# The heads' projection of a two-block model on one core: six accumulation banks filled slice by slice, and the vector engine's side work in another order

## What is computed

```python
y_b = hgrn2_mixer(p[..., o1:o2], p[..., o2:o3], p[..., o3:o4], p[..., o4:o5], lower_bounds[l], hgrn_norm_g[l])
merged = (jax.nn.sigmoid(p[..., o5:o6]) * (y_a @ w_ssm_proj[l])
          + jax.nn.sigmoid(p[..., o6:]) * (y_b @ w_hgrn_proj[l]))
```

## Time and profile before

| what | value |
|---|---|
| median of the runs | 3601.41 us |
| the profiled execution, its own time | 3603.62 us |
| span of the profiled execution | 3601.8 us |
| TensorE matmul busy | 3289.2 us, 91% |
| VectorE / ScalarE / GpSimd busy | 56% / 26% / 6% |
| mean granted TensorE clock | 0.946 of full |
| stage `heads_out`, first to last matmul | 933.15 to 1056.39 us |

### The profile page before, as it was taken

The page is one execution under the profiler, slowest core; times in us unless marked ns, Lnnn a source line. Parts: engine busy times, 40 slices in busy tenths (PEclk is TensorE's granted clock), DMA queues, the critical chain, the costliest instruction groups (busy, mean ns, idle before and its releaser), DMA issues. The chain is left out here.

```text
span 3601.8 us, 47693 instructions
## 1 busy us (share of the span) xinstructions
PE 3289.2 (91%) x20158; PEld 3042.2 (84%) x20158; DVE 2008.2 (56%) x2814; ACT 943.8 (26%) x1178; POOL 227.4 (6%) x224
## 2 busy tenths in 40 slices
PE   3999999999688779999999999899988996988887
PEld 3999999999677679999999999899988983555465
DVE  5565655566568444566446446645445535666446
ACT  3222222222323331121111111221133314444323
POOL 0000000000005200000000000000012000222200
PEclk9999999999798789999999999999989997999898
DMA  3222222222343344321321321411121321000031
GB/s 100 91 78 75 90 85 86 90 89 74 137 102 50 95 170 135 129 77 53 106 81 46 108 79 38 153 37 43 50 74 37 128 87 74 1 1 1 22 133 69
DMA packets 102463, 285.76 MB, mean 79 GB/s; under 512 B 13157, under 2 KB 32101, under 8 KB 101993
## 3 DMA queue, kind: packets, MB, share of 16 engines
q1 hardware_dynamic: 102248, 282.70, 24.6%
HBM read 218.68 MB, written 63.98 MB: 78 GB/s over the span
## 5 line engine op out<-in xcount | busy, mean ns | idle before, releaser
L491 PE MATMUL mixer_in_dense<-mix_z_high,mixer_in_whigh 128*128 128x348 f32 x1344 | 445.8, 332 | 11.3 <-POOL mixer_in_out L328 11.3
L491 PE MATMUL mixer_in_dense<-mix_z_high,mixer_in_wlow 128*128 128x348 f32 x1344 | 439.1, 327 | 0.0
L491 PE MATMUL mixer_in_dense<-mix_z_low,mixer_in_whigh 128*128 128x348 f32 x1344 | 438.2, 326 | 0.0
L1372 PE MATMUL flow_dense<-rst_norms_operand_b_high,flow_whigh 128*128 128x342 f32 x1248 | 399.2, 320 | 0.4 <-DVE flow_wlow L1464 0.4
L1372 PE MATMUL flow_dense<-irst_norms_operand_b_low,flow_whigh 128*128 128x342 f32 x1248 | 398.3, 319 | 0.0
L1372 PE MATMUL flow_dense<-rst_norms_operand_b_high,flow_wlow 128*128 128x342 f32 x1248 | 397.4, 318 | 0.0
L1930 PE MATMUL joint_dense<-rst_norms_operand_b_high,joint_whigh 128*128 128x342 f32 (+2 forms) x1056 | 344.7, 326 | 17.0 <-DVEq L2047 10.1
L1930 PE MATMUL joint_dense<-rst_norms_operand_b_high,joint_wlow 128*128 128x342 f32 (+2 forms) x1056 | 341.7, 324 | 0.0
L1930 PE MATMUL joint_dense<-irst_norms_operand_b_low,joint_whigh 128*128 128x342 f32 (+2 forms) x1056 | 340.6, 323 | 0.0
L1372 PE MATMUL flow_dense<-first_operand_a_high,flow_whigh 128*128 128x342 f32 (+1 forms) x912 | 291.4, 320 | 26.9 <-DVEq L1485 26.9
L1372 PE MATMUL flow_dense<-first_operand_a_low,flow_whigh 128*128 128x342 f32 (+1 forms) x912 | 291.8, 320 | 0.0
(11 more groups left out here) (544 smaller groups left out, 6201.3 us busy)
## 6 DMA issues: line engine op xcount, KB each, us to landing
mixer_in_wstage<-w_in SPq DMA_DIRECT2D x56, 512.0 KB, 4.6
mixer_in_mod_w<-w_mod SPq DMA_DIRECT2D x64, 384.0 KB, 3.6
first_norms_weights<-w_up SPq DMA_DIRECT2D x44, 512.0 KB, 3.5
flow_side<-h SPq DMA_DIRECT2D x24, 512.0 KB, 4.3
h<-flow_out SPq DMA_DIRECT2D x24, 512.0 KB, 3.2
first_norms_weights<-ab_w_in SPq DMA_DIRECT2D x20, 512.0 KB, 3.6
p<-mixer_in_out SPq DMA_DIRECT2D x16, 528.0 KB, 2.9
first_norms_weights<-w_down SPq DMA_DIRECT2D x16, 512.0 KB, 3.5
```

Of the source, the lines that this page charges most:

```text
L491: mm = pe.matmul(pd[s % 2][:, 0:W], a[n % 2][:, P * m:P * (m + 1)], z[x][:, m, W * b:W * (b + 1)], start=m == 0 and i == 0, stop=m == DT - ...
L1372: mm = pe.matmul(o, w[n % NW][:, P * k:P * (k + 1)], x[h][:, k, where], start=k == 0 and e == 0, stop=k == kt - 1 and e == 2)
```

## The change

It keeps every operation and changes places:

1. TensorE begins with six slices at once, the two first output tiles: for each block k it makes the three matmuls of each of the slices 0 to 5, in six banks (`RING` is 6). The slices from 6 on are made one by one, as before.
2. So `high(1)` and `low(1)` move to the front, ahead of the split of block 1, and the load of weight tile 1 moves ahead of the load of block 1. `high` and `low` of the tiles from 2 on stay where they were, `low(2)` at s = 4.
3. The table of pieces: one power behind each of blocks 4 to 6 and four behind block 7 (it was two each, and one). `turns` to `vectors` are one slice later; `table` 0 goes from s = 3 (ahead of the gate of tile 1 and of `high(2)` on ScalarE) to s = 4 (behind both), `table` 1 from s = 6 to s = 7 (behind the gate of tile 2 and `high(3)`). `outer` 1 goes from 7 to 8, `outer` 6 from 16 to 15.

```diff
-    W, NP, NQ, RING = NM // 3, NPAIR, 8, 4
+    W, NP, NQ, RING = NM // 3, NPAIR, 8, 6
...
-    for s, name, k in ((-8, "step", 0), (-7, "angles", 0), (-5, "base", 0), (-4, "power", 2), (-4, "power", 3),
...
+    for s, name, k in ((-8, "step", 0), (-7, "angles", 0), (-5, "base", 0), (-4, "power", 2), (-3, "power", 3),
...
@@ SyncE
                 for m in range(4):
                     load_yb(m)
+                    if m == 0:
+                        load(1)
                 for m in range(4, HH):
                     sp.wait_ge(x_low, m - 3)
                     load_yb(m)
-                load(1)
@@ ScalarE
                 high(0)
                 for m in range(HH):
+                    if m == 1:
+                        high(1)
...
-                        if n + 1 < DT:
+                        if n and n + 1 < DT:
                             high(n + 1)
@@ TensorE
-                for s in range(NS):
...
+                def products(s, k):
                     n, b = divmod(s, 3)
+                    for e, (w, v) in enumerate(((wh, 0), (wl, 0), (wh, 1))):
+                        mm = pe.matmul(pd[s % RING][:, 0:W], w[n % 2][:, P * k:P * (k + 1)],
+                                       x[v][:, k, FIRST + W * b:FIRST + W * (b + 1)],
+                                       start=k == 0 and e == 0, stop=k == DT - 1 and e == 2)
+                    return mm
+
+                for k in range(DT):
+                    pe.wait_ge(x_low, k + 1)
+                    for s in range(6):
+                        if k == 0 and s % 3 == 0:
+                            pe.wait_ge(low_ready, s // 3 + 1)
+                        mm = products(s, k)
+                        if k == DT - 1:
+                            mm.then_inc(full, 1)
+                for s in range(6, NS):
+                    if s % 3 == 0:
+                        pe.wait_ge(low_ready, s // 3 + 1)
+                    pe.wait_ge(moved, s - RING + 1)
                     for k in range(DT):
+                        mm = products(s, k)
                     mm.then_inc(full, 1)
@@ VectorE
                 low(0)
                 for m in range(HH):
+                    if m == 1:
+                        low(1)
...
-                    if b == 1 and n + 1 < DT:
+                    if n and b == 1 and n + 1 < DT:
                         low(n + 1)
```

More of the change, by code:

```diff
@@ L650, in heads_out @@
     at = {}
-    for s, name, k in ((-8, "step", 0), (-7, "angles", 0), (-5, "base", 0), (-4, "power", 2), (-4, "power", 3),
[L652 to L655, removed]
+    for s, name, k in ((-8, "step", 0), (-7, "angles", 0), (-5, "base", 0), (-4, "power", 2), (-3, "power", 3),
+                       (-2, "power", 4), (-1, "power", 5), (-1, "power", 6), (-1, "power", 7), (-1, "power", 8),
+                       (1, "turns", 0), (2, "rotation", 0), (2, "reverse", 0), (3, "coefficients", 0), (4, "table", 0),
+                       (5, "negate", 0), (5, "scaled_b", 0), (6, "vectors", 0), (7, "table", 1), (8, "outer", 1),
+                       (9, "outer", 2), (11, "outer", 3), (12, "outer", 4), (14, "outer", 5), (15, "outer", 6),
                        (17, "outer", 7), (19, "outer", 8), (20, "outer", 0), (21, "skip", 0)):
@@ L784, in _ @@
             def _(pe):
-                for s in range(NS):
+                def products(s, k):
                     n, b = divmod(s, 3)
[L787 to L790, removed]
-                    for k in range(DT):
[L792 to L797, removed]
+                    for e, (w, v) in enumerate(((wh, 0), (wl, 0), (wh, 1))):
[15 more added lines that the diff above has]
+                    pe.wait_ge(moved, s - RING + 1)
+                    for k in range(DT):
+                        mm = products(s, k)
                     mm.then_inc(full, 1)
```

## The result

The change takes 3577.99 us (median of 12 runs, 3569.66 to 3587.96), the kernel before, in as many runs beside it, 3598.04 (3591.66 to 3604.99). The ratio is 0.9945, interval 0.9934 to 0.9957: 20.1 us faster, between 15.5 and 23.7. The forecast was 3585.7 with a range from 3580 to 3593, and a gain of 15.7.

The account below looks back on a forecast made before the run. The prediction took TensorE's stream and its breaks as the bound. Slice 6 starting 9.3 us earlier plus 6.2 from the second break made 15.5; counted the other way 15.7, which was taken: 3601.41 - 15.7 = 3585.7 us, range 3580 to 3593.

Parts of the forecast that it names:

- The front: TensorE's first six slices, block by block: slice 0 full 22.1 us after the first matmul, block waits costed at nothing.
- the twin in `flow`: Stage `flow` already starts with six slices over six banks; its 22.1 us for 129 matmuls was taken over.
- The second rival: TensorE's first six slices stay at 1.2 GHz: 3601.5 us, no change; chance 0.05 with other partial clock losses.
- would keep the lower clock: What the skill page's rule would mean for the first six slices; the prediction said the trace disagrees, 1.00 over 22.5 us.
- VectorE up to `low(2)`: VectorE's row of work from slice 0 full at 955.3 us: 15.35 us together, `low(2)` done at 970.65.
- the wait of 13 us: TensorE stands from 957.7 to 970.7 us for `low(2)`, replacing the slow slice 0 and the 7.99 us wait.
- From slice 6 on: TensorE's remaining slices: `low(3)` ready at 982.7, needed at 984.3, so the second break's 6.2 us are gained.
- second wait: TensorE's later wait for `wlow` in the kernel before, 4.54 us until 998.39; forecast to vanish.
- the margin: VectorE's time in hand when `low(3)` is done before TensorE reaches tile 3: 1.6 us.
- The restart: TensorE's loss at low clock after its long wait: 2.3 us, allowed to be 1.7 or 2.3.
- The rest: Banks, stores, gate loads and the scan behind the stage: no cost, the scan starting from the same state, only earlier.
- The base of the number: The median before, 3601.41 us of three runs spread over 7 us, taken to carry perhaps 2 us.

Follow-up runs that it names:

- e2_tables: The kernel before, still slice after slice, with only the pieces from `turns` on moved as in the change: 3576.66 us, ratio 0.9952.
- e3: The changed kernel with its six-bank start, but the whole table of pieces, powers included, as in the kernel before: 3596.76 us, ratio 1.0006.
- e10_best_slices: The kernel before, slice after slice with six banks, with a table of pieces made for that order: 3574.88 us.

## Why the prediction was right in the stage and wrong in the number

- *The front:* right. 22.1 us to the first full slice as read off the twin in `flow`, no wait for a block, clock up after some 3 us. The second rival (the clock stays down while banks are switched) is out: 1.00 over 18.2 us of the front. The Trainium skill, page "TensorE: Matmul & The Clock Gate", section "A second HAM failure mode: psum-queue depth-cycling", puts such a swing of the clock down to short idles of TensorE between groups of matmuls. This front has none (busy 18.20 of 18.20 us), so it shows that changing banks alone leaves the clock up; it doesn't test the page's cause, and the prediction's "would keep the lower clock" took more from the page than it says.
- *VectorE up to `low(2)`:* right to 0.1 us (37.6 against 37.5 from the first matmul), and so was the wait of 13 us. But by e2_tables this path, and not the front, is what moved slice 6 forward.
- *From slice 6 on:* no second wait, as said; the margin is 1.3 to 1.4 us, not 1.6. The restart was mis-sized: 2.3 us by the first restart of before, 1.5 here (clock 0.69 over 5 us), outside the "1.7 or 2.3" that was allowed. That is the 0.8 between 15.7 and the measured 16.5.
- *"The rest"*, costed at nothing: this step failed. 3.5 us of the measured gain (4.4 and 2.7 in the repetitions) lie outside the stage. Each of these is about as large as its interval; the three together are clear of zero. Every operation there is the same. What the profiles show in its place is time that varies between executions: the clock falls at more or fewer places in the input projection (6.8 to 17.1 us lost), the attention takes 432.1 to 439.7 us, and the last stage waits 12.7 to 14.7 us at its start. Why the change comes out 3.5 us better in this is open.
- *The base of the number* failed as well: "the median carries perhaps 2 us". Three runs gave 3601.41; twelve gave 3598.04, and later sets 3594.0 to 3594.6. Of the 7.7 us between forecast and result 3.4 are this, 0.8 the restart, and about 3.5 the rest of the program. Either of the two without the other would have left the result inside the range. As a difference, 15.7 lies just inside the measured 15.5 to 23.7, and near its low end because of the restart and the rest.
- *What the working did not say:* it put the front and the pieces in one sum. The same rows would have told that without the new order of pieces the front only lengthens a wait (e3), and that without the front `low(2)` would have come as early (37.7 us behind the first matmul in e2_tables, 37.6 in the change) and TensorE would just have been busy until then. The 13 us wait that was forecast was the sign: time won ahead of a wait whose end another engine sets is not won.

## What to carry to other kernels

When a change has two parts, walk the releasing engine's row with each part alone: a faster arrival at a wait is worth nothing until the work that ends the wait is earlier, and here four lines of a table did all of it. Then look at what still stands ahead of the late operation and is not needed there: with `rotation`, `coefficients` and `table` 0 moved behind it and the rest spread anew, the stage lost another 10 us. Check the total too: of these 10 us some 2 arrived there, for a reason that stays open. And a forecast of a small change belongs on the difference of two kernels run side by side: three runs of this 3.6 ms program lay 3.4 us over the median of twelve and 7 over those of later sets, in a range 13 wide.

## What the runs showed of the hardware

The granted clock falls in code without a single wait of TensorE in the trace: 6.8 to 17.1 us lost in 840 us of the input projection, four to ten times about 1.7 us, at recurring places, taken or not from execution to execution, which moves the start of a later stage by 10 us (923.2 to 933.2). A front with short waits kept 1.2 GHz for 18 us in e10_best_slices and for 22 in e2_tables, while six slices at once, without waits, had 2.4 GHz after some 3 us in the change; that, beside the waits themselves, is what the slice-by-slice start costs.
